# Splitting an expert's first overflow block over two steps of a mixture-of-experts loop

## The chip, the cores and the metric

One core of one Trainium2 chip runs the whole program. The number that counts is the device time of one execution in microseconds (us); lower is better. Engines are named as the profile names them: PE (TensorE, matrix products), DVE (VectorE), ACT (ScalarE), POOL (GpSimd), SP (SyncE, which here only issues the weight transfers).

## What is computed

One decoder layer on 256 tokens of width 1024: a mixer of three kinds of attention, a layer norm, then a mixture of experts (top 4 of 32) and a second layer norm. The change touches the experts alone:

```python
D_MODEL = D_EXPERT = 1024; SEQ = 256; N_EXPERTS = 32; TOP_K = 4      # all float32

def moe_ffn(h, router_w, router_b, w_gu, b_gu, w_dn, b_dn):
    logits = h @ router_w + router_b
    top_logit, top_e = lax.top_k(logits, TOP_K)
    top_w = softmax(top_logit)
    # for every expert e, over the tokens that chose it:
    gu = x @ w_gu[e] + b_gu[e]                      # 1024 -> 2048
    gate = minimum(gu[:, :1024], 7.0)
    up = clip(gu[:, 1024:], -7.0, 7.0)
    act = gate * sigmoid(1.702 * gate) * (up + 1.0)
    y = act @ w_dn[e] + b_dn[e]                     # 1024 -> 1024
    out[tokens] += y * w                            # weighted, added to each token's row
```

The weights of one expert are 8.39 MB (gate and up) and 4.19 MB (down). All 32 are read once, 403 MB in all.

## The kernel before

**Tiling.** An expert has 64 slots for its tokens. An expert chosen by more than 64 tokens has the others done in overflow blocks of 32 slots (`XSLOTS`); `nx[e]` holds how many such blocks expert e needs, and every engine reads it into a register and branches on it. The trace shows two overflow blocks: one for expert 1 (from 298 us) and one for expert 15 (from 741 us), counting from 0.

**Loop.** A pass of the loop (`Fori(0, PAIRS - 1)`, 15 passes) takes two experts: in the first half PE runs the gate-up of expert 2i+1, the gathers for the next two, the down product of 2i, the overflow blocks of 2i, and the transposes of the activations of 2i+1. In the second half it runs the gate-up of 2i+2, the down product of 2i+1, the overflow blocks of 2i+1 (`extra_blocks(1, ...)`, L1130 region), the transposes, and `combine`, which adds the two outputs into four PSUM banks.

**An overflow block on PE** is a gather (`extra_gather`, into PSUM bank PB6), the gate-up (`extra_gate_up_chunk`, 4 chunks, into PB6), transposes of routing weights and activations, the down product (`extra_down_chunk`, 4 chunks), and a combine. DVE makes its one-hot rows (`extra_one_hots`, L1509 to L1520) and its activations (L1494 to L1500 with 64 partitions), ACT copies.

**Weight buffers and the transfer queue.** There are two buffers for gate-up weights (`gu_slot[0]` even experts, `gu_slot[1]` odd ones) and one for down weights (`dn_slot`). SP issues all transfers in one fixed order, expert by expert: gate-up of e+2 (L325), then down of e+1 (L330), each in 4 chunks. A chunk of gate-up e+2 waits for `guc` (the expert's own gate-up has read the chunk of e) and for `xguc` (so have its overflow blocks). A chunk of down e+1 waits for `dn_used` and `xdnc` in the same way. So in the old order an overflow block of e holds the gate-up buffer of e until the next expert's gate-up and the down product of e are through.

**Names in the rows.** `WB` are the weight buffers, `S` (S1, S2) and `K` work tiles and constants in SBUF, `X` the tokens, `PB` the eight PSUM banks. All matrix products are recorded by one helper line, L713 in the kernel before; in the trace every float32 product is two MATMUL rows. L1044 are the transposes of activations, L1087 those of an overflow block, L1538 DVE's copy of the down output.

Of the kernel before, what the change touches and what calls it, by code (L numbers as in the profile page):

```python
# [13 lines left out]
P = 128  # L14
# [40 lines left out]
def hybrid_layer(nc, x, w_in, b_in, pos_k, pos_v, w1_k, w2_k, w1_v, w2_v, g_out, w_out, ln1_g, ln1_b,  # L55
                 router_w, router_b, w_gu, b_gu, w_dn, b_dn, ln2_g, ln2_b, out):
    with ExitStack() as ctx:
# [427 lines left out]
        def _(act):  # L485
# [144 lines left out]
            def extra_slots():  # L630

                act.reg_add(xcount, xcount, 1)
                xc = act.snap(xcount, min_val=1, max_val=96)
                act.wait_ge(s["xga"], xc)
                act.activation(yx[:, 0:KT * XSLOTS], PB[6][:, 0:KT * XSLOTS], ACT.Copy).then_inc(s["xxg"], 1)
# [38 lines left out]
            def extra_blocks(t):  # L674
                n = act.value_load(nx[0:1, t:t + 1] if isinstance(t, int) else nx[0:1, bass.ds(t, 1)], min_val=0,
                                   max_val=MAX_EXTRA)
                with act.If(n > 0):
                    with act.Fori(0, n):
# [8 lines left out]
            combine_weights(1)  # L687
            with act.Fori(0, PAIRS - 1) as i:
                sigmoid(2 * i + 2)
                slots_to_sbuf(0, 6, 2 * i + 3)  # L690
                slots_to_sbuf(1, 4, 2 * i + 4)
                expert_output(0, 2 * i + 1)
                extra_blocks(2 * i)
                act_columns(6, 2 * i + 2)
                sigmoid(2 * i + 3)
                expert_output(1, 2 * i + 2)
                extra_blocks(2 * i + 1)
                act_columns(5, 2 * i + 3)
                combine_weights(i + 2)
            sigmoid(N_EXPERTS)  # L700
            expert_output(0, N_EXPERTS - 1)
            extra_blocks(N_EXPERTS - 2)
            act_columns(6, N_EXPERTS)
            expert_output(1, N_EXPERTS)
            extra_blocks(N_EXPERTS - 1)
# [3 lines left out]
        def _(pe):  # L709
# [357 lines left out]
            def extra_gather(outputs_copied):  # L1067

                pe.reg_add(xcount, xcount, 1)
                xc = pe.snap(xcount, min_val=1, max_val=96)  # L1070

                pe.wait_ge(s["ysb_ok"], outputs_copied + 1)
                pe.wait_ge(s["ysb_dv"], outputs_copied)
                pe.wait_ge(s["xoh"], xc)
                for k in range(KT):
                    for b in range(TB):
                        ins = mm(PB[6][:, XSLOTS * k:XSLOTS * k + XSLOTS], x_sb[:, b, P * k:P * k + P], ohx[:, b, :],
                                 k == 0 and b == 0, b == TB - 1)
                ins.then_inc(s["xga"], 1)
                pe.wait_ge(s["xxg"], xc)  # L1080

# [19 lines left out]
            def extra_blocks(e, t, n):  # L1101

                count = pe.value_load(nx[0:1, t:t + 1] if isinstance(t, int) else nx[0:1, bass.ds(t, 1)], min_val=0,
                                      max_val=MAX_EXTRA)
                with pe.If(count > 0):
                    with pe.Fori(0, count):
                        extra_gather(n)
                        for c in range(GU_CHUNKS):
                            extra_gate_up_chunk(c, e).then_inc(s["xguc"], 1)
                        extra_gate_up_bias(e).then_inc(s["xgu"], 1)  # L1110
                        extra_act_transposes()
                        xc = pe.snap(xcount, min_val=1, max_val=96)
                        pe.wait_ge(s["xctd"], xc)
                        pe.wait_ge(s["xactT"], xc)
                        for c in range(DN_CHUNKS):
                            extra_down_chunk(c).then_inc(s["xdnc"], 1)
                        extra_combine()
                pe.nop()
# [33 lines left out]

            pe.wait_ge(s["actT"], N_EXPERTS - 1)
            gate_up(1, PAIRS, N_EXPERTS)
            pe.wait_ge(s["ct_sb"], PAIRS)
            down(0, PAIRS, N_EXPERTS - 1)
            extra_blocks(0, N_EXPERTS - 2, N_EXPERTS - 1)
            act_transposes(6, N_EXPERTS)
            down(1, PAIRS, N_EXPERTS)
            extra_blocks(1, N_EXPERTS - 1, N_EXPERTS)  # L1160
# [6 lines left out]
        def _(dve):  # L1167
# [372 lines left out]
            def extra_blocks(t, activations_done):  # L1540
                at = (lambda a: a[:, t:t + 1, :]) if isinstance(t, int) else (lambda a: a[:, bass.ds(t, 1), :])
                n = dve.value_load(nx[0:1, t:t + 1] if isinstance(t, int) else nx[0:1, bass.ds(t, 1)], min_val=0,
                                   max_val=MAX_EXTRA)
                with dve.If(n > 0):
# [3 lines left out]
                    with dve.Fori(0, n):  # L1548
                        extra_one_hots()
                        extra_activations(activations_done)  # L1550
# [13 lines left out]
            expert_activations(1)  # L1564
            next_one_hots(0)
            with dve.Fori(0, PAIRS - 1) as i:
# [11 lines left out]
            extra_blocks(N_EXPERTS - 2, N_EXPERTS)  # L1578
            expert_output(1, N_EXPERTS)
            extra_blocks(N_EXPERTS - 1, N_EXPERTS)  # L1580
# [36 lines left out]
```

## Time and profile before

| | |
|---|---|
| median of 3 runs | 1245.11 us (1243.04 to 1245.42) |
| the profiled execution's own time | 1245.07 us |
| its span in the trace | 1243.3 us |
| PE busy | 1115.8 us, 90% |
| DVE, ACT, POOL busy | 266.8, 146.3, 29.7 us |
| moved by DMA | 426.18 MB, 343 GB/s over the span |

The engines' busy times are sums over stages with different limits. The 40 slices show the DMA engines full from about 310 us to the end, but for slices 23 and 24, and empty in part of the stretch before 310 us. The chain that ended last names PE's products with 47% and gate-up transfers with 22% of the span: it goes over PE after each overflow block and over the transfers in between.

### The profile page before, as it was taken

The page shows a single profiled execution, that of the slowest core. Times are in us where ns is not written, and L with a number is a line of the kernel's source. Part 1 is how long each engine was busy: PE and PEld are TensorE (multiplying, and loading weights), DVE is VectorE, ACT ScalarE, POOL GpSimd, SP SyncE. Part 2 cuts the span into 40 slices and gives each one's busy share as a digit, 9 for nine tenths or more (in the row PEclk, how much of TensorE's full clock was granted, in tenths as well). Part 3 has the DMA queues.
Part 4 walks back from the last instruction along what each step waited for, and adds up shares of the span by engine and source line. Part 5 has one row for each costly group of instructions (what it writes and reads, how often), then busy time and mean ns, then how long its engine had stood idle before and what let it go on. Part 6 is the DMA issues. An engine that isn't in the chain of part 4 may idle for free.

```text
span 1243.3 us, 14596 instructions
## 1 busy us (share of the span) xinstructions
PE 1115.8 (90%) x5388; PEld 489.2 (39%) x5389; DVE 266.8 (21%) x767; ACT 146.3 (12%) x309; POOL 29.7 (2%) x52
## 2 busy tenths in 40 slices
PE   7999796998899999999999978999999999999983
PEld 6677445334243333333333333434333332323321
DVE  2353535111112111120211111111212111111113
ACT  2043311100000110000100001000010010100000
POOL 2000410000000000000000000000000000000000
PEclk9999896997999999999999998999999999999997
DMA  9400849630999999999999957999999999999992
GB/s 315 180 1 1 269 196 395 273 137 2 408 418 418 418 418 418 419 418 418 418 418 418 418 243 314 418 418 418 418 418 418 418 419 418 418 418 418 418 414 119
DMA packets 80386, 426.18 MB, mean 343 GB/s; under 512 B 6009, under 2 KB 7594, under 8 KB 47562
## 3 DMA queue, kind: packets, MB, share of 16 engines
q1 hardware_dynamic: 79834, 425.37, 84.7%
q10 hardware_dynamic: 528, 0.48, 0.1%
q8 instruction: 16, 0.26, 0.1%
q14 instruction: 8, 0.07, 0.0%
HBM read 424.78 MB, written 1.05 MB: 343 GB/s over the span
## 4 chain that ended last, share of the span: by engine, by line
PE 49%; DMA 25%; SPq 18%; DVE 3%; issue 3%; ACT 1%; POOL 0%; DVEq 0%; POOLq 0%; ACTq 0%
PE PB L713 47%; DMA WB<-in_w_gate_up_dram 22%; SPq L330 11%; SPq L325 6%; DMA WB<-in_w_down_dram 3%; PE PB L1044 0%; DMA X<-in_x_dram 0%; SPq L334 0%; DVE S L1391 0%; PE PB L720 0%; DVE S L1520 0%; POOL K L476 0%; DVE WB L1285 0%; PE PB L803 0%; DVE S L1497 0%
## 5 line engine op out<-in xcount | busy, mean ns | idle before, releaser
L713 PE MATMUL PB<-WB,S 128*64 128x512 f32 (+5 forms) x3472 | 770.5, 596 | 60.6 <-DMA WB<-in_w_gate_up_dram 54.3
L713 PEld LDWEIGHTS PB<-WB,S 128*64 128x64 f32 (+2 forms) x3472 | 253.2, 140 | 541.7 <-issue 413.4
L1494 DVE TENSOR_SCALAR S<-PB 128x512 f32<-128x512 f32 (+1 forms) x34 | 23.5, 691 | 617.2 <-PE PB L713 617.2
L713 PE MATMUL PB<-S 128*64 128x512 f32 (+5 forms) x464 | 138.2, 580 | 4.7 <-issue 2.3
L656 ACT ACTIVATE S<-S 128x512 f32<-128x512 f32 x32 | 20.2, 630 | 568.7 <-DVE S L1494 568.7
L713 PE MATMUL PB<-S,X 128*128 128x128 f32 (+1 forms) x576 | 76.9, 295 | 9.3 <-DVE S L1520 8.0
L713 PEld LDWEIGHTS PB<-S,X 128*128 128x128 f32 x576 | 73.6, 211 | 23.7 <-issue 21.9
L713 PEld LDWEIGHTS PB<-S 128*64 128x64 f32 (+4 forms) x464 | 53.0, 167 | 74.4 <-issue 67.4
L1538 DVE COPY S<-PB 64x512 f32<-64x512 f32 x32 | 21.9, 684 | 197.6 <-PE PB L713 197.6
L713 PE MATMUL PB<-S,WB 128*128 128x256 f32 (+2 forms) x336 | 63.2, 388 | 0.4 <-ACT S L496 0.4
L713 PEld LDWEIGHTS PB<-S,WB 128*128 128x128 f32 (+1 forms) x336 | 49.1, 177 | 12.4 <-issue 2.1
L713 PE MATMUL PB<-WB 128*32 128x128 f32 (+7 forms) x260 | 44.6, 361 | 5.2 <-DVE WB L1358 3.3
L672 ACT ACTIVATE S<-PB 64x512 f32<-64x512 f32 x32 | 19.0, 594 | 194.9 <-PE PB L713 194.9
L713 PEld LDWEIGHTS PB<-WB 128*64 128x64 f32 (+2 forms) x260 | 27.4, 152 | 18.7 <-issue 13.7
L480 POOL TENSOR_TENSOR K<-K 128x1 f32<-128x1 f32 x2 | 3.0, 1512 | 1041.6 <-DVE K L1413 1041.6
L1044 PEld LDWEIGHTS PB<-K,S 128*128 128x128 f32 x128 | 13.4, 140 | 30.8 <-issue 27.0
L1044 PE MATMUL PB<-K,S 128*128 128x128 f32 x128 | 21.0, 287 | 4.8 <-DVE S L1500 2.8
L1497 DVE SCALAR_TENSOR_TENSOR S<-S 128x512 f32<-128x512 f32 (+1 forms) x34 | 23.5, 691 | 1.2
L1500 DVE TENSOR_TENSOR S<-S 128x512 f32<-128x512 f32 (+1 forms) x34 | 23.5, 691 | 1.2
L1495 DVE TENSOR_SCALAR S<-PB 128x512 f32<-128x512 f32 (+1 forms) x34 | 23.1, 681 | 0.1
L622 ACT ACTIVATE S<-PB 128x512 f32<-128x512 f32 x32 | 19.1, 597 | 32.9 <-PE PB L713 32.9
L1469 DVE TENSOR_SCALAR S<-K 128x64 f32<-128x64 f32 x68 | 16.9, 249 | 20.6 <-PE PB L1049 19.1
(198 smaller groups left out, 338.0 us busy)
## 6 DMA issues: line engine op xcount, KB each, us to landing
WB<-in_w_gate_up_dram SPq DMA_DIRECT2D x128, 2048.0 KB, 22.8
WB<-in_w_down_dram SPq DMA_DIRECT2D x128, 1024.0 KB, 22.9
WB<-in_w_in_dram SPq DMA_DIRECT2D x1, 3088.0 KB, 16.0
WB<-in_w_in_dram SPq DMA_DIRECT2D x1, 3072.0 KB, 20.7
WB<-in_w_in_dram SPq DMA_DIRECT2D x1, 2144.0 KB, 10.8
WB<-in_w_in_dram SPq DMA_DIRECT2D x1, 2048.0 KB, 15.8
WB<-in_w_out_dram SPq DMA_DIRECT2D x2, 1024.0 KB, 10.3
WB<-in_w_out_dram SPq DMA_DIRECT2D x1, 2048.0 KB, 16.8
```

The costliest lines, as they stand in the source:

```text
L325: sp.dma_start(gu_slot[par][:, kk * c:kk * c + kk, :], src[:, kk * c:kk * c + kk, :]).then_inc(s_gul[par][c], 16)
L330: sp.dma_start(dn_slot[:, kk * c:kk * c + kk, :], src[:, kk * c:kk * c + kk, :]).then_inc(s_dnl[par][c], 16)
L622: act.activation(xg[:, 4 * h:4 * h + 4, :].rearrange("p k s -> p (k s)"), PB[bank][:, :], ACT.Copy)\
L656: act.activation(act_sb, gt, ACT.Sigmoid, scale=SWIGLU_ALPHA).then_inc(s["sig"], 1)
L672: act.activation(ysb[64 * e:64 * e + 64, 1, :], PB[7][64:128, :], ACT.Copy).then_inc(s["ysb_ok"], 1)
L713: return mm_(o, l, r, start=start, stop=stop, skip_group_check=True)
L1044: ins = tr(PB[bank][:, P * c:P * c + P], act_sb[:, P * c:P * c + P], ident)
L1494: ts(g, gate, LIMIT, None, ALU.min).then_inc(s[g_ok], 1)
L1495: ts(u, up, LIMIT, -LIMIT, ALU.min, ALU.max).then_inc(s[clip], 1)
L1497: stt(u, u, 1.0, g, ALU.add, ALU.mult).then_inc(s[upg], 1)
L1500: tt(a, u, a, ALU.mult).then_inc(s[done], 1)
L1538: cp(ysb[64 * e:64 * e + 64, 0, :], PB[7][0:64, :]).then_inc(s["ysb_dv"], 1)
```

## The change

The first overflow block of an expert is split. Gather, gate-up and activations now stand at the end of the step in which the expert's own gate-up ran (`start_extra_block`); transposes, down product and combine stay where the whole block stood (`end_extra_blocks`), and blocks after the first are still run there whole. The gather goes to bank PB4 instead of PB6. The main gather's first half moves from PB6 to PB7, so `down` now waits for its copy (`xg_ok`), and the wait for `ct_sb` moves behind it. PE, ACT and DVE each get one more read of `nx` and two more branches per expert. DVE's activations of an expert get a wait for those of the overflow block.

```diff
@@ PE
-            def extra_gather(outputs_copied):
+            def extra_gather():
...
-                pe.wait_ge(s["ysb_ok"], outputs_copied + 1)
-                pe.wait_ge(s["ysb_dv"], outputs_copied)
                 pe.wait_ge(s["xoh"], xc)
...
-                        ins = mm(PB[6][:, XSLOTS * k:XSLOTS * k + XSLOTS], x_sb[:, b, P * k:P * k + P], ohx[:, b, :],
+                        ins = mm(PB[4][:, XSLOTS * k:XSLOTS * k + XSLOTS], x_sb[:, b, P * k:P * k + P], ohx[:, b, :],
...
+            def start_extra_block(e, t, pb6_copied, copies):
+                n = extra_count(t)
+                with pe.If(n > 0):
+                    extra_gather()
+                    pe.wait_ge(s[pb6_copied], copies)
+                    extra_gate_up(e)
+                pe.nop()
+
+            def end_extra_blocks(e, t, outputs_copied):
+                n = extra_count(t)
+                with pe.If(n > 0):
+                    pe.wait_ge(s["ysb_ok"], outputs_copied + 1)
+                    pe.wait_ge(s["ysb_dv"], outputs_copied)
+                    extra_act_transposes()
+                    extra_down()
+                    extra_combine()
+                pe.nop()
+                with pe.If(n > 1):
+                    with pe.Fori(1, n):
+                        extra_gather()
+                        extra_gate_up(e)
                         extra_act_transposes()
+                        extra_down()
                         extra_combine()
                 pe.nop()
...
             combine()
+            start_extra_block(0, 0, "ct_sb", 1)
             with pe.Fori(0, PAIRS - 1) as i:
                 pe.wait_ge(s["actT"], 2 * i + 1)
                 gate_up(1, i + 1, 2 * i + 2)
                 pe.wait_ge(s["ohs"], i + 2)
-                pe.wait_ge(s["ct_sb"], i + 1)
-                gather(0, 6)
+                gather(0, 7)
                 pe.wait_ge(s["g_ok"], 2 * i + 2)
                 gather(1, 4)
+                pe.wait_ge(s["xg_ok"], 2 * i + 3)
                 down(0, i + 1, 2 * i + 1)
                 pe.wait_ge(s["xg_ok"], 2 * i + 4)
-                extra_blocks(0, 2 * i, 2 * i + 1)
+                end_extra_blocks(0, 2 * i, 2 * i + 1)
+                pe.wait_ge(s["ct_sb"], i + 1)
                 act_transposes(6, 2 * i + 2)
+                start_extra_block(1, 2 * i + 1, "actT", 2 * i + 2)
                 gate_up(0, i + 2, 2 * i + 3)
                 down(1, i + 1, 2 * i + 2)
-                extra_blocks(1, 2 * i + 1, 2 * i + 2)
+                end_extra_blocks(1, 2 * i + 1, 2 * i + 2)
                 act_transposes(5, 2 * i + 3)
                 weight_transposes()
                 pe.wait_ge(s["ysb_ok"], 2 * i + 3)
                 pe.wait_ge(s["ysb_dv"], 2 * i + 2)
                 combine()
+                start_extra_block(0, 2 * i + 2, "ct_sb", i + 2)
@@ DVE
             def expert_activations(n):
+                dve.wait_ge(s["xact"], dve.snap(dve.snap(xcount, min_val=0, max_val=96) + 1, min_val=1, max_val=97))
                 dve.wait_ge(s["gu"], n)
...
             with dve.Fori(0, PAIRS - 1) as i:
                 expert_activations(2 * i + 2)
                 expert_output(0, 2 * i + 1)
-                extra_blocks(2 * i, 2 * i + 2)
+                end_extra_blocks(2 * i, 2 * i + 2)
                 next_expert_rows(0, 2 * i + 1)
+                start_extra_slots(2 * i + 1)
+                start_extra_block(2 * i + 1, 2 * i + 2)
                 expert_activations(2 * i + 3)
                 expert_output(1, 2 * i + 2)
-                extra_blocks(2 * i + 1, 2 * i + 3)
+                end_extra_blocks(2 * i + 1, 2 * i + 3)
                 next_expert_rows(1, 2 * i + 2)
+                start_extra_slots(2 * i + 2)
                 next_one_hots(i + 1)
+                start_extra_block(2 * i + 2, 2 * i + 3)
```

ACT is split in the same way: it copies the gathered rows (`extra_slots`) and takes the sigmoid in `start_extra_block`, after `act_columns`, and the other copies in `end_extra_blocks`. SP is unchanged.

**PE, first half of a pass, before.** Behind the down product of the even expert (PB7) come the read of `nx`, the branch, and the whole overflow block; its gate-up is the 32 products into PB6.

```order
L713 MATMUL PB7<-WB,S2 64x512 x16
L1140 REGISTER_ALU
L1103 ISA
L1103 TENSOR_LOAD nx
L1103 ISA x2
L1105 COMPARE_AND_BRANCH
L1106 UNCONDITIONAL_BRANCH
L1069 ISA
L713 MATMUL PB6<-S2,X 128x32 x16
L713 MATMUL PB6<-WB,S2 32x512 x32
L713 MATMUL PB6<-S1,S2 32x512 x4
L1083 ISA
```

**PE, middle of a pass, after.** Behind the transposes of the odd expert's activations (L1062), and ahead of the next expert's gate-up (PB4, last row):

```order
L1062 MATMUL PB6<-K,S2 128x128 x4
L1129 ISA
L1129 TENSOR_LOAD nx
L1129 ISA x2
L1135 COMPARE_AND_BRANCH
L1087 ISA
L731 MATMUL PB4<-S2,X 128x32 x16
L731 MATMUL PB6<-WB,S2 32x512 x32
L731 MATMUL PB6<-S1,S2 32x512 x4
L1135 UNCONDITIONAL_BRANCH
L1027 REGISTER_ALU
L731 MATMUL PB4<-WB,S2 64x512 x2
```

The gate-up of the odd expert's overflow block has moved ahead of the next expert's gate-up and of its own expert's down product.

**DVE, second half of a pass, before**: the read of `nx` and the one-hot rows follow the copy of the odd expert's own down output.

```order
L1538 COPY S2<-PB7 64x512
L1542 TENSOR_LOAD nx
L1542 ISA x2
L1544 COMPARE_AND_BRANCH
L1545 TENSOR_SCALAR K<-K 128x2
L1546 COPY K<-K 128x2
L1547 REGISTER_ALU
L1548 UNCONDITIONAL_BRANCH
L1509 ISA
L1514 REGISTER_ALU
L1515 TENSOR_SCALAR K<-K 128x2
L1518 TENSOR_SCALAR S2<-K 128x32
```

**DVE, first half of a pass, after**: they follow the small operations for the next expert's bias rows (L1523, L1519), which themselves follow the copy of the even expert's down output.

```order
L1523 TENSOR_SCALAR K<-K 128x1
L1519 TENSOR_SCALAR S2<-K 128x64
L1588 REGISTER_ALU
L1588 TENSOR_LOAD nx
L1588 ISA x2
L1595 COMPARE_AND_BRANCH
L1596 ISA
L1596 TENSOR_SCALAR K<-K 128x2
L1597 ISA
L1597 COPY K<-K 128x2
L1598 ISA
L1559 REGISTER_ALU
```

So the odd expert's one-hot rows are made half a pass earlier, behind the copy of the expert before it.

## Rows read from the trace of the kernel before

**Rows 1.** The page's 40 slices of the span: GB/s moved by DMA.

```profile
GB/s 315 180 1 1 269 196 395 273 137 2 408 418 418 418 418 418 419 418 418 418 418 418 418 243 314 418 418 418 418 418 418 418 419 418 418 418 418 418 414 119
```

**Rows 2.** Windows: us, busy time by engine, PE clock, DMA share, GB/s.

```profile
276.50:309.50 33.00, 28.53 (x136) 13.60 (x136) 5.87 (x18) 1.61 (x3) 0.00 (x0) 0.82 0.00 1
...
320.00:733.00 413.00, 385.54 (x1832) 144.29 (x1834) 64.95 (x164) 37.32 (x65) 0.00 (x0) 1.00 1.02 418
...
735.00:752.00 17.00, 12.54 (x64) 8.22 (x64) 3.21 (x14) 0.98 (x2) 0.00 (x0) 0.70 0.00 0
```

**Rows 3.** PE timeline around expert 15's block: start, us, what [idle before, releaser].

```profile
711.48 7.15 PE L713 MATMUL PB<-WB,S 128*64 128x512 f32 x32
...
730.12 7.04 PE L713 MATMUL PB<-WB,S 128*64 128x512 f32 x32
741.14 6.84 PE L713 MATMUL PB<-S,X 128*128 128x32 f32 x32 [3.98 <-DVE S L1520]
...
760.98 0.44 PE L1087 MATMUL PB<-K,S 128*128 128x128 f32 x2 [3.08 <-DVE S L1500]
...
793.63 6.66 PE L713 MATMUL PB<-WB,S 128*64 128x512 f32 x30
```

**Rows 4.** SP's transfer issues around both blocks (L325 gate-up, L330 down weights).

```profile
309.75 6.42 SPq L325 DMA_DIRECT2D WB<-in_w_gate_up_dram  x4
322.54 4.28 SPq L330 DMA_DIRECT2D WB<-in_w_down_dram  x4
```

```profile
752.12 5.50 SPq L325 DMA_DIRECT2D WB<-in_w_gate_up_dram  x4
764.49 3.47 SPq L330 DMA_DIRECT2D WB<-in_w_down_dram  x4
...
795.88 3.76 SPq L330 DMA_DIRECT2D WB<-in_w_down_dram  x3
```

**Rows 5.** PE timeline: the loop's start, expert 1's block, a pass behind it, the end.

```profile
241.22 13.95 PE L713 MATMUL PB<-WB,S 128*64 128x512 f32 x64
...
269.60 0.66 PE L1044 MATMUL PB<-K,S 128*128 128x128 f32 x4 [1.92 <-issue]
270.19 15.65 PE L713 MATMUL PB<-WB,S 128*64 128x512 f32 x64
...
298.42 7.00 PE L713 MATMUL PB<-S,X 128*128 128x32 f32 x32 [4.00 <-DVE S L1520]
...
319.53 0.44 PE L1087 MATMUL PB<-K,S 128*128 128x128 f32 x2 [3.08 <-DVE S L1500]
```

```profile
352.49 7.09 PE L713 MATMUL PB<-WB,S 128*64 128x512 f32 x32
359.51 0.66 PE L1044 MATMUL PB<-K,S 128*128 128x128 f32 x4
...
387.12 13.95 PE L713 MATMUL PB<-WB,S 128*64 128x512 f32 x64
...
402.72 3.84 PE L713 MATMUL PB<-S,X 128*128 128x128 f32 x32
406.49 7.09 PE L713 MATMUL PB<-WB,S 128*64 128x512 f32 x32
...
1201.54 3.60 PE L713 MATMUL PB<-WB,S 128*64 128x512 f32 x16
```

**Rows 6.** DVE timeline ahead of expert 15's block: output copy, last one-hot rows.

```profile
737.20 0.69 DVE L1538 COPY S<-PB 64x512 f32<-64x512 f32 x1 [4.13 <-PE PB L713]
...
740.07 0.92 DVE L1520 TENSOR_SCALAR S<-K 128x32 f32<-128x32 f32 x4
```

**Rows 7.** Instruction queue: whole span, 200 to 345 us; then every queue of 345 to 1195 us.

```profile
q8 instruction: 16, 0.26, 0.1%
```

```profile
q8 instruction: 6, 0.10, 0.3%
```

```profile
q1 hardware_dynamic: 59630, 346.55, 99.3%
```

More of the change, by code:

```diff
@@ L634, in extra_slots @@
                 act.wait_ge(s["xga"], xc)
-                act.activation(yx[:, 0:KT * XSLOTS], PB[6][:, 0:KT * XSLOTS], ACT.Copy).then_inc(s["xxg"], 1)
+                act.activation(yx[:, 0:KT * XSLOTS], PB[4][:, 0:KT * XSLOTS], ACT.Copy).then_inc(s["xxg"], 1)
             def extra_sigmoid():
@@ L672, in expert_output, with extra_count, start_extra_block, end_extra_blocks @@
                 act.activation(ysb[64 * e:64 * e + 64, 1, :], PB[7][64:128, :], ACT.Copy).then_inc(s["ysb_ok"], 1)
-            def extra_blocks(t):
-                n = act.value_load(nx[0:1, t:t + 1] if isinstance(t, int) else nx[0:1, bass.ds(t, 1)], min_val=0,
-                                   max_val=MAX_EXTRA)
-                with act.If(n > 0):
-                    with act.Fori(0, n):
+            def extra_count(t):
+                return act.value_load(nx[0:1, t:t + 1] if isinstance(t, int) else nx[0:1, bass.ds(t, 1)], min_val=0,
+                                      max_val=MAX_EXTRA)
+            def start_extra_block(t):
+                n = extra_count(t)
+                with act.If(n > 0):
+                    extra_slots()
+                    extra_sigmoid()
+                act.nop()
+            def end_extra_blocks(t):
+                n = extra_count(t)
+                with act.If(n > 0):
+                    extra_act_copy()
+                    extra_outputs()
+                act.nop()
+                with act.If(n > 1):
+                    with act.Fori(1, n):
                         extra_slots()
@@ L1080, in extra_gather, with extra_gate_up, extra_down @@
                 pe.wait_ge(s["xxg"], xc)
+            def extra_gate_up(e):
+                for c in range(GU_CHUNKS):
+                    extra_gate_up_chunk(c, e).then_inc(s["xguc"], 1)
+                extra_gate_up_bias(e).then_inc(s["xgu"], 1)
+            def extra_down():
+                xc = pe.snap(xcount, min_val=1, max_val=96)
+                pe.wait_ge(s["xctd"], xc)
+                pe.wait_ge(s["xactT"], xc)
+                for c in range(DN_CHUNKS):
+                    extra_down_chunk(c).then_inc(s["xdnc"], 1)
             def extra_act_transposes():
@@ L1099, in extra_combine, with extra_count @@
                         mm(acc(b, h)[:, :], CTx[64 * h:64 * h + 64, b, :], yx[64 * h:64 * h + 64, :], False, False)
[L1101 to L1110, printed above, removed]
-                        extra_act_transposes()
[L1112 to L1116, printed above, removed]
+            def extra_count(t):
+                return pe.value_load(nx[0:1, t:t + 1] if isinstance(t, int) else nx[0:1, bass.ds(t, 1)], min_val=0,
+                                     max_val=MAX_EXTRA)
+            def start_extra_block(e, t, pb6_copied, copies):
+                n = extra_count(t)
+                with pe.If(n > 0):
[4 more added lines that the diff above has]
+            def end_extra_blocks(e, t, outputs_copied):
+                n = extra_count(t)
+                with pe.If(n > 0):
[9 more added lines that the diff above has]
+                        extra_gate_up(e)
+                        extra_act_transposes()
+                        extra_down()
                         extra_combine()
@@ L1547, in extra_blocks, with start_extra_block, end_extra_blocks @@
                     dve.reg_add(xexperts, xexperts, 1)
-                    with dve.Fori(0, n):
+                    extra_one_hots()
+                dve.nop()
+            def start_extra_block(t, activations_done):
+                n = extra_count(t)
+                with dve.If(n > 0):
+                    extra_activations(activations_done)
+                dve.nop()
+                dve.nop()
+            def end_extra_blocks(t, activations_done):
+                n = extra_count(t)
+                with dve.If(n > 1):
+                    with dve.Fori(1, n):
                         extra_one_hots()
@@ L1564, in _ @@
             expert_activations(1)
+            start_extra_slots(0)
             next_one_hots(0)
+            start_extra_block(0, 1)
             with dve.Fori(0, PAIRS - 1) as i:
```

35 lines of the change are left out of this document (22 added, 13 removed).

## The prediction, as it stood before the run

> **What bounds the kernel now.** I read the 40 slices first. From slice 10 on the DMA engines are full at 418 GB/s, except in slices 23 and 24 [rows 1]. Windows set around the holes show the rest: 418 GB/s from 320 to 733 us and, by the slices, the same behind 754.5 us; nothing from 276.5 to 309.5 and from 735 to 752 us [rows 2]. So the end is set by the weight stream: its volume at 418 GB/s, plus the time in which it stands still. One expert's weights (12.58 MB) take 30.1 us, 20.1 of them gate-up (8.39 MB) and 10.0 down. PE has slack: unhindered it does a pass of two experts in 406.49 - 352.49 = 54.0 us [rows 5] against 60.2 for the stream.
>
> Both holes belong to the overflow blocks. SP issues the gate-up load of expert e+2 only when the block of e has read the buffer: at 309.75 and 752.12 us [rows 4], 11.3 and 11.0 us after the block's gather began [rows 3, 5]; data flow about 1.1 us after an issue. By edges of the windows I take the stream as dead from 275.3 to 310.8 us (35.5 us, expert 1) and from 734.0 to 753.2 us (19.2 us, expert 15).
>
> **What the change does at expert 15.** It moves the block's gather and gate-up ahead of the gate-up of 16, which starts at 711.48 [rows 3]. All times are in the clock of the old trace.
> - DVE must first make the one-hot rows. From the start of its output copy to the last one takes 740.99 - 737.20 = 3.8 us [rows 6]; two small operations for the bias rows now stand between, some 0.5 us. The down product of 14 ends 0.6 us of transposes before 711.48 and its copy starts near 711.0, so PE can gather from 715.4. PE is idle 4 us, as now (3.98). I cost this at the same slow gather as today: the clock in 735 to 752 us is 0.70 on average [rows 2], so part of it ran at 1.2 GHz, and the same idle should bring the same.
> - Gather to end of gate-up takes 760.98 - 3.08 - 741.14 = 16.8 us [rows 3]: PE is free at 732.2.
> - SP issues the load for 17 at 715.4 + 11.0 = 726.4. The stream is still busy until 734.0, so this hole closes, and the load is through at 754.1.
> - But down of 16 also waits (`xdnc`) for the block's down product. PE: gate-up of 16 without waits 402.72 - 387.12 = 15.6 [rows 5], down of 15 7.0, a copy of 0.7 [rows 6] that the block's transposes must now await. They start at 755.5 instead of 760.98, 5.5 us earlier. The issue of down 16 moves from 764.49 [rows 4] to 759.0, its data to 760.1: a new hole of 6.0 us. Hidden now: the wait of 3.08 us for DVE's activations, and the DMA-paced part of the gate-up.
> - Next late is down of 17, issued once down 16 has run: 795.88 [rows 4] minus 5.5, data at 791.5. The stream, from 760.1 on with 30.1 us of work, is out at 790.2: 1.3 us more.
> In the kernel before, the stream reaches that load at 753.2 + 20.1 + 30.1 = 803.4. **Gain 803.4 - 791.5 = 11.9 us**, not the 19.2 us of the hole: the limit becomes PE's own path over the block. Further on PE takes 27.0 us for an expert against 30.1, so no hole follows.
>
> **At expert 1.** The down product of 0 ends 1.92 us before 269.60 [rows 5]; with 4.3 us of DVE work and 0.3 for its slower first pass PE gathers from 272.3. The block runs 319.53 - 3.08 - 298.42 = 18.0 us, to 290.3; gate-up 15.6, down 7.0, copy 0.7: transposes at 313.6 instead of 319.53. That is 5.9 earlier; 1.5 of it because the gate-up of 2 ran partly at half clock behind the 1.92 us stop (15.65 us for its 64 products, against 13.95 at 387.12). The load of 3 is issued at 272.3 + 11.3 = 283.6 (data 284.7 to 304.8), down of 2 at 322.54 - 5.9 = 316.6 (data 317.7 to 347.8, with gate-up of 4). Down of 3 waits for down of 2, at 352.49 [rows 5] plus the 2.25 us from start to issue seen at 793.63 and 795.88 [rows 3, 4]: 354.7 - 5.9 + 1.1 = 349.9. Before, the stream is there at 310.8 + 50.2 = 361.0. **Gain 11.1 us**.
>
> **What it costs.** The moved waits are free: down waits for ACT's copy of the first gather half (a bank's copy, 0.7 us on DVE [rows 6]), which the second half of the 3.84 us gather covers [rows 5]; without that cover it would cost 0.7 us per pass, within the slack. PE gets one more read of `nx` and two more branches per expert. In the steady passes the present read and branch cost PE nothing visible: down starts at 352.49 and lasts 7.09, transposes follow at 359.51 [rows 5]. In the first pass the same place shows 1.92 us of "issue" [rows 5]. Bounds for an added branch are thus 0 and 1.92 us; below nothing is excluded, since nothing is removed. I take 0 in steady state (the nearest row, and the slack covers small stops), 1 us in each of the two catch-up stretches, and 3 us at the end, where the code behind the loop is run once and two added skips stand ahead of the last down product. Sum: 11.9 + 11.1 - 2 - 3 = 18, of which I drop 1 for ends rounded in my favour. 1245.07 (the profiled execution, which lies within 0.1 us of the median) - 17 = **1228 us**.
>
> **The rule that speaks against it.** PE's code in the loop grows: by the built order 290 matrix products before, 446 after, since gather, gate-up, down and combine now stand twice per expert. With two MATMUL and two weight loads for each float32 product that is about 1160 and 1790 instructions. The instruction queue q8 brings 16 packets in the span, 6 of them between 200 and 345 us, and none from 345 to 1195 us, where only q1 moved anything [rows 7]: the old loop was loaded once and stayed. Whether the new one does, no row shows. The Trainium skill ("Runtime: NRT & Kernel Launch", Instruction fetch mechanics) says that PE holds 2048 instructions in 16 KiB blocks of 256, refilled first in, first out with sequential prefetch, and that a taken branch to a block that isn't there stalls for the fetch. By that page, as an estimate, the new loop covers all eight blocks and the prefetched ninth would push out the first; the trace agrees with the page on the block size (0.26 MB in 16 packets).
>
> **Rivals.**
> 1. *The loop no longer stays loaded and the skips stop PE, slower.* The place is the branches over unused code: five per pass (one long one behind each of the two down products, one over the unused first half behind each set of transposes, one back to the loop's start). PE alone would finish at 358 + 15p us: the first gate-up of the loop starts at 241.2 and the down product behind the last one at 1201.5 [rows 5], 43.6 before the end; between them 15 passes of p, the last gate-up of 15.6, and an estimated 29 for each block (its 18.0 and 16.8, and 12 for transposes, down, combine and the idle ahead). At p = 59.1 this is the old time, so it decides from 5.1 us of stops per pass. Three stops of 1.92 give 59.8 and 1255 us; five 63.6 and 1312; with a half-clock gate-up behind two of them (1.7 each) 67.0 and 1363. For it: code 1.5 times as long, and a first pass that shows the stop. 
> 2. *Small stops eat the gain.* One refetch per pass and 3 us of idle with its half clock makes p 58.7 to 59.3, where PE and no longer the stream is the bound: 1238 to 1248.
> 3. *Both holes close wholly*: 35.5 + 19.2 = 55 us less, 1190 to 1210. For it: gate-up loads are two thirds of the stream. Against it: `xdnc` still ties the down weights to the late half of the block.
>
> **How the numbers follow.** Forecast (gain 7 to 31, 1214 to 1238): 0.55. The low end is both blocks at full clock and no branch cost, the high end both added branches visible. Rival 1: 0.28, spread over 1255 to 1360. Rival 2: 0.12. Rival 3: 0.05. The range from 1213 to 1300 holds the forecast, rival 2 and nearly half of rival 1, together 0.8. A change of 0.2% (2.5 us) is about what a measurement of this kernel can tell from none. Faster: 0.55 + 0.05 + 0.05 of rival 2; same 0.03; slower 0.32.
>
> **What would show it.** Right: gate-up load of 3 issued near 284 and of 17 near 726; holes of about 9 and 13 us around expert 1, and of 6 to 8 us near 755 (all later times shifted by the first gain); 418 GB/s elsewhere; q8 with no packets through the loop, or one or two per pass; PE waits for gate-up chunks again before the end. Wrong: q8 with dozens of packets, "issue" stops of 2 us and more behind the down products, a DMA rate under 418 GB/s throughout. If the holes close to 5 us or less in sum, the PE path was costed too long.

## The result, and the profile after

The changed kernel takes 1417.38 us (median of 4, 1415.85 to 1421.1) against 1244.07 for the kernel before beside it: ratio 1.140, 95% interval 1.138 to 1.143. The forecast was 1228 with a range of 1213 to 1300; the time is 173 us longer than before and outside it. The profiled execution has a span of 1413.9 us and a mean PE clock of 0.89 (0.97 before). Lines have moved: products are L731 (was L713), the transposes of the activations L1062 (L1044) and of the one-hot rows L1067 (L1049), the block's transposes L1114 (L1087), DVE's output copy L1585 (L1538) and block one-hot rows L1565 (L1520), the last activation step L1545 (L1500).

The page's 40 slices answer [rows 1]:

```profile
GB/s 323 112 1 94 237 380 286 120 238 359 326 385 321 390 339 381 327 388 313 388 319 382 195 264 295 378 338 369 347 360 356 357 359 356 361 351 364 340 189 131
```

There is no plateau at 418 GB/s left. The blocks show as dips (120 and 238 GB/s in slices 8 and 9, 195 and 264 in slices 23 and 24), but the slices between them run at 313 to 390. So the stream no longer sets the end. The page says who does: its queue row (packets, MB, share), the chain that ended last by engine, and the costliest group (busy, mean ns | idle before, releaser).

```profile
q8 instruction: 147, 2.41, 0.8%
...
PE 81%; issue 14%; DVE 3%; DMA 1%; ACT 1%; SPq 0%; POOL 0%; DVEq 0%; POOLq 0%; ACTq 0%
...
L731 PE MATMUL PB<-WB,S 128*64 128x512 f32 (+5 forms) x3472 | 820.0, 631 | 156.6 <-issue 153.2
```

The instruction queue brought 147 packets, where it brought 16 [rows 7]. PE stood for 153.2 us ahead of its products without waiting for any semaphore, and 14% of 1413.9 us, 198 us, of the chain is such time.

The PE timeline shows where. It starts at the overflow block of expert 1 and runs through the first two steady passes (start, us, what, [idle before, releaser]), for [rows 5]:

```profile
271.55 0.63 PE L1062 MATMUL PB<-K,S 128*128 128x128 f32 x4 [2.06 <-issue]
...
274.80 7.03 PE L731 MATMUL PB<-S,X 128*128 128x32 f32 x32 [2.62 <-DVE S L1565]
...
315.60 0.43 PE L1114 MATMUL PB<-K,S 128*128 128x128 f32 x2 [0.98 <-DVE S L1585]
...
353.52 3.84 PE L731 MATMUL PB<-S,X 128*128 128x128 f32 x32
357.29 7.09 PE L731 MATMUL PB<-WB,S 128*64 128x512 f32 x32
366.35 0.63 PE L1062 MATMUL PB<-K,S 128*128 128x128 f32 x4 [1.97 <-issue]
372.05 15.38 PE L731 MATMUL PB<-WB,S 128*64 128x512 f32 x64 [5.07 <-issue]
...
406.54 16.89 PE L731 MATMUL PB<-WB,S 128*64 128x512 f32 x64 [5.99 <-issue]
...
425.08 3.84 PE L731 MATMUL PB<-S,X 128*128 128x128 f32 x32
...
438.01 0.63 PE L1062 MATMUL PB<-K,S 128*128 128x128 f32 x4 [2.07 <-issue]
443.65 15.41 PE L731 MATMUL PB<-WB,S 128*64 128x512 f32 x64 [5.01 <-issue]
...
477.38 15.62 PE L731 MATMUL PB<-WB,S 128*64 128x512 f32 x64 [5.18 <-issue]
...
494.64 3.84 PE L731 MATMUL PB<-S,X 128*128 128x128 f32 x32
```

A pass now takes 425.08 - 353.52 = 71.6 us, where PE alone took 54.0 and the stream 60.2. The 17.6 us are three stops, 1.97 + 5.07 + 5.99 = 13.0, and the two gate-ups behind the long ones, of which a part runs at half clock: 15.38 and 16.89 us (granted clock 0.90 and 0.82) where 13.95 is the full-clock time [rows 5], 1.4 + 2.9. All three lie where a skip jumps over unused code: behind the first down product, behind the transposes of the odd expert's activations, and at the loop's end. Behind the second down product there are skips too, and no stop shows. The next pass has the same three and takes 69.6 us. Rival 1's formula, 358 + 15p, gives 1402 to 1432 for these two passes; the span is 1413.9.

The middle of the run as one window, 345 to 1150 us (us, busy time of PE, its weight loads, DVE, ACT and POOL, then PE clock, DMA share, GB/s), where [rows 2] had 418 GB/s:

```profile
345.00:1150.00 805.00, 662.67 (x2970) 251.11 (x2966) 109.52 (x281) 59.76 (x104) 0.00 (x0) 0.89 0.86 342
```

And PE's groups in that window: first the products, then the transposes (busy, mean ns of one | idle before, releaser).

```profile
L731 PE MATMUL PB<-WB,S 128*64 128x512 f32 (+1 forms) x2190 | 520.4, 649 | 114.8 <-issue 113.7 <-ACT S L647 0.6 <-ACT S L635 0.5
...
L1062 PE MATMUL PB<-K,S 128*128 128x128 f32 x88 | 14.1, 283 | 22.9 <-issue 22.9
```

In the kernel before, the same group of products has its idle time from the weights, 49.0 of 50.0 us, and none from issue:

```profile
L713 PE MATMUL PB<-WB,S 128*64 128x512 f32 (+1 forms) x2626 | 576.8, 601 | 50.0 <-DMA WB<-in_w_gate_up_dram 49.0 <-ACT S L647 0.6 <-ACT S L635 0.5
```

**The theory from here** (A): the larger PE loop is fetched anew in each pass, and the skips wait for it. **Rivals**: (B) the added reads of `nx` and branches themselves cost this, wherever the code lies; (C) the moved waits or the split itself set the pass.

### The profile page after: what moved, and what is told of

Same layout as the page of the kernel before. It is cut to its first block, busy times and chain, and to the rows that moved or that the text cites. A ratio compares the mean times of both kernels' runs of the same rounds, so it can differ in the third digit from the quotient of the medians.

```text
span 1413.9 us, 15234 instructions
## 1 busy us (share of the span) xinstructions
PE 1167.7 (83%) x5388; PEld 510.7 (36%) x5389; DVE 267.3 (19%) x767; ACT 146.2 (10%) x309; POOL 29.7 (2%) x52
## 3 DMA queue, kind: packets, MB, share of 16 engines
q8 instruction: 147, 2.41, 0.8%
## 4 chain that ended last, share of the span: by engine, by line
PE 81%; issue 14%; DVE 3%; DMA 1%; ACT 1%; SPq 0%; POOL 0%; DVEq 0%; POOLq 0%; ACTq 0%
PE PB L731 78%; PE PB L1062 1%; DMA WB<-in_w_in_dram 1%; DVE S L1436 0%; PE PB L1067 0%; POOL K L476 0%; DVE S L1565 0%; SPq L304 0%; DVE WB L1330 0%; DVEq L1588 0%; DVE S L1585 0%; PE PB L821 0%; SPq L312 0%; DVE K L1454 0%; PE PB L962 0%
## 5 line engine op out<-in xcount | busy, mean ns | idle before, releaser
L731 PE MATMUL PB<-WB,S 128*64 128x512 f32 (+5 forms) x3472 | 820.0, 631 | 156.6 <-issue 153.2
L731 PEld LDWEIGHTS PB<-WB,S 128*64 128x64 f32 (+2 forms) x3472 | 274.9, 150 | 668.8 <-issue 660.6
L731 PE MATMUL PB<-S 128*64 128x512 f32 (+5 forms) x464 | 138.8, 582 | 3.2 <-ACT S L652 1.4
L731 PE MATMUL PB<-S,X 128*128 128x128 f32 (+1 forms) x576 | 77.2, 296 | 6.2 <-DVE S L1565 4.8
L731 PEld LDWEIGHTS PB<-S,X 128*128 128x128 f32 x576 | 73.9, 212 | 19.3 <-issue 12.2
L731 PEld LDWEIGHTS PB<-S 128*64 128x64 f32 (+4 forms) x464 | 53.4, 168 | 73.2 <-issue 64.6
L731 PE MATMUL PB<-S,WB 128*128 128x256 f32 (+2 forms) x336 | 61.8, 383 | 0.7 <-ACT S L496 0.5
L1585 DVE COPY S<-PB 64x512 f32<-64x512 f32 x32 | 21.9, 683 | 202.3 <-PE PB L731 202.3
L731 PEld LDWEIGHTS PB<-S,WB 128*128 128x128 f32 (+1 forms) x336 | 47.8, 174 | 12.4 <-issue 2.1
L1062 PE MATMUL PB<-K,S 128*128 128x128 f32 x128 | 21.0, 288 | 36.1 <-issue 33.1
L731 PE MATMUL PB<-WB 128*32 128x128 f32 (+7 forms) x260 | 44.7, 362 | 5.2 <-DVE WB L1403 3.3
L1062 PEld LDWEIGHTS PB<-K,S 128*128 128x128 f32 x128 | 13.7, 143 | 62.6 <-issue 58.8
L731 PEld LDWEIGHTS PB<-WB 128*64 128x64 f32 (+2 forms) x260 | 27.5, 152 | 18.7 <-issue 13.7
L660 ACT ACTIVATE S<-PB 128x512 f32<-128x512 f32 x32 | 19.1, 597 | 45.1 <-PE PB L1062 45.1
L1545 DVE TENSOR_TENSOR S<-S 128x512 f32<-128x512 f32 (+1 forms) x34 | 23.5, 691 | 1.2
L622 ACT ACTIVATE S<-PB 128x512 f32<-128x512 f32 x32 | 19.1, 597 | 33.0 <-PE PB L731 33.0
```

The costliest lines, as they stand in the source:

```text
L622: act.activation(xg[:, 4 * h:4 * h + 4, :].rearrange("p k s -> p (k s)"), PB[bank][:, :], ACT.Copy)\
L660: act.activation(actT[:, :, :].rearrange("p c s -> p (c s)"), PB[bank][:, :], ACT.Copy)\
L731: return mm_(o, l, r, start=start, stop=stop, skip_group_check=True)
L1062: ins = tr(PB[bank][:, P * c:P * c + P], act_sb[:, P * c:P * c + P], ident)
L1545: tt(a, u, a, ALU.mult).then_inc(s[done], 1)
L1585: cp(ysb[64 * e:64 * e + 64, 0, :], PB[7][0:64, :]).then_inc(s["ysb_dv"], 1)
```

## The experiments

A count is used in them: PE instructions by the built program, with four for a float32 product (two MATMUL, two weight loads) and two for a transpose. The loop has 1163 before and 1790 after. The queue's packets are 16 KB each (2.41 MB in 147). I count the code in blocks of 256 instructions; that is what the Trainium skill says ("Runtime: NRT & Kernel Launch", Instruction fetch mechanics) of 16 KiB, and the 16 KB packets agree with it.

**e1: only the first block, split.** The loops for second and later blocks are left out on PE; with these inputs they never run. The split stays, the loop shrinks to 1168 instructions.

```diff
 def end_extra_blocks(e, t, outputs_copied):
     ...
     pe.nop()
-    with pe.If(n > 1):
-        with pe.Fori(1, n):
-            extra_gather()
-            extra_gate_up(e)
-            extra_act_transposes()
-            extra_down()
-            extra_combine()
-    pe.nop()
```

> The changed kernel without PE's code for overflow blocks after the first (it is never run with these inputs, where no expert has more than one). The loop's code falls from about 1790 to 1168 PE instructions; reads of nx and the first branches stay. Theory A (the loop's code no longer stays loaded): the stops of 5 to 6 us per half pass vanish, q8 brings nothing from about 345 us to the end of the loop, and the time is 1222 to 1233 us, which is also where the split alone should land. Theory B (the added reads and branches themselves stop PE, four reads instead of two per pass): 1390 us or more. Theory C (the split order makes PE wait for DVE or ACT in every pass): unchanged at 1417.

Measured: 1223.07 us (4 runs), ratio 0.982 [0.977, 0.986]. The stops are gone: 0 packets on q8 in the window 345 to 1150 us, and the products wait for weights again:

```profile
L731 PE MATMUL PB<-WB,S 128*64 128x512 f32 (+1 forms) x2672 | 586.8, 603 | 40.7 <-DMA WB<-in_w_gate_up_dram 39.6 <-ACT S L647 0.6 <-ACT S L635 0.5
```

So (C) falls: split, waits and reads are as in the changed kernel. What is missing is unused code and the test `n > 1` ahead of it, one skip per expert; whether that skip matters is for e4 and e5. This kernel also shows the forecast's own terms. PE's timeline at the loop's start and around both blocks:

```profile
239.61 5.94 PE L731 MATMUL PB<-S 128*128 128x512 f32 x8
245.48 13.95 PE L731 MATMUL PB<-WB,S 128*64 128x512 f32 x64
...
277.25 7.04 PE L731 MATMUL PB<-S,X 128*128 128x32 f32 x32 [4.73 <-DVE S L1557]
...
318.06 0.43 PE L1114 MATMUL PB<-K,S 128*128 128x128 f32 x2 [0.98 <-DVE S L1577]
...
708.85 7.04 PE L731 MATMUL PB<-S,X 128*128 128x32 f32 x32 [4.42 <-DVE S L1557]
...
750.60 0.43 PE L1114 MATMUL PB<-K,S 128*128 128x128 f32 x2 [0.98 <-DVE S L1577]
```

SP's issues of gate-up and down weights, as in [rows 4]:

```profile
288.62 5.72 SPq L325 DMA_DIRECT2D WB<-in_w_gate_up_dram  x4
...
320.70 2.95 SPq L330 DMA_DIRECT2D WB<-in_w_down_dram  x4
...
720.22 6.66 SPq L325 DMA_DIRECT2D WB<-in_w_gate_up_dram  x4
...
753.25 4.63 SPq L330 DMA_DIRECT2D WB<-in_w_down_dram  x4
```

Windows in the holes and between them:

```profile
280.50:289.50 9.00, 8.53 (x46) 4.88 (x50) 0.00 (x0) 0.38 (x1) 0.00 (x0) 0.55 0.00 0
312.20:321.60 9.40, 7.86 (x51) 2.77 (x51) 2.17 (x7) 1.36 (x3) 0.00 (x0) 1.00 0.01 2
345.00:745.00 400.00, 374.82 (x1808) 144.64 (x1806) 67.99 (x172) 35.99 (x62) 0.00 (x0) 0.98 1.02 416
747.50:754.00 6.50, 4.95 (x32) 1.76 (x32) 1.40 (x5) 1.36 (x3) 0.00 (x0) 0.92 0.00 0
```

**e2: the old kernel with unused code.** The kernel before, plus a branch never taken over two more gate-ups, once per half pass: 1743 instructions, and nothing split or moved.

```diff
 (kernel before, in the extra blocks' code, once per expert)
+with pe.If(count > 5):
+    for c in range(GU_CHUNKS):
+        extra_gate_up_chunk(c, e)
+    extra_gate_up_bias(e)
+    for c in range(GU_CHUNKS):
+        extra_gate_up_chunk(c, e)
+    extra_gate_up_bias(e)
```

> The kernel before, order untouched, with a never-taken branch of 288 PE instructions after each pair of overflow blocks (1743 instructions in the loop instead of 1163, over 8 blocks of 256). Theory A: about nine packets of q8 per pass, PE's pass near 65 to 71 us, 1335 to 1425 us. Theories B and C: 1244 us, since only one more branch per half pass is run and no order changes.

Measured: 1445.43 us (2 runs), ratio 1.161 [1.155, 1.167], 20 us above what I expected at most. The direction is (A)'s: unused code, with one skip per half pass over it, makes the old kernel slower than the changed one. PE's timeline has the same kind of stop, here the longest behind a down product, and the queue row of 345 to 1150 us shows the fetches:

```profile
365.85 7.09 PE L713 MATMUL PB<-WB,S 128*64 128x512 f32 x32
380.39 1.12 PE L1044 MATMUL PB<-K,S 128*128 128x128 f32 x4 [7.46 <-issue]
...
407.66 0.66 PE L1044 MATMUL PB<-K,S 128*128 128x128 f32 x4 [1.98 <-issue]
```

```profile
q8 instruction: 95, 1.56, 0.8%
```

**e4: the old kernel with more reads and branches, little code.** This is (B) by itself: per half pass two more reads of `nx`, each with a branch not taken; 1247 instructions.

```diff
+for _ in range(2):
+    again = pe.value_load(nx[...], min_val=0, max_val=MAX_EXTRA)
+    with pe.If(again > 5):
+        extra_gate_up_bias(e)
+    pe.nop()
```

> The kernel before with two more reads of nx and two more never-taken short branches per half pass on PE (1247 instructions in the loop). Theory A: 1243 to 1246 us, no stop on PE. Theory B: four more reads and branches per pass at the 1 to 2 us of the stops seen give 1260 to 1330 us.

Measured: 1247.82 us (8 runs), ratio 1.0030 [1.0009, 1.0052], 2 us above my range. The total alone proves little, since the stream hides up to 60.2 - 54.0 = 6.2 us per pass. PE's own pass decides: where it has no wait for weights (from one first down product to the next) it takes 409.73 - 355.74 = 54.0 us, as before. But where PE waits for weights anyway, one small stop per pass does show, 0.4 to 0.9 us behind the second down product, against my "no stop on PE"; in 345 to 1150 us, with no packet on q8, they add up to:

```profile
L1044 PE MATMUL PB<-K,S 128*128 128x128 f32 x104 | 17.1, 287 | 7.2 <-issue 7.1
```

The changed kernel has 113.7 + 22.9 us of issue idle in its window. So (B) falls as the cause: four reads and branches more per pass cost 0.9 us of PE's time at most where their code is held.

**e3, e6: the changed kernel with shorter code.** The second copy of the block is saved by turning the loop around: one body ends a block and begins the next. It does as many blocks as the changed kernel's. 1602 instructions. e3 has some 100 unused instructions ahead of the loop besides, e6 none.

```diff
-    with pe.If(n > 0):
-        waits, act_transposes, down, combine
-    with pe.If(n > 1):
-        with pe.Fori(1, n):
-            gather, gate_up(e), act_transposes, down, combine
+    with pe.If(n > 0):
+        with pe.Fori(0, n) as j:
+            waits, act_transposes, down, combine
+            with pe.If(j < n - 1):
+                gather, gate_up(e)
```

> The changed kernel with the code for later blocks folded: one loop over all blocks of an expert, transposes, down and combine first, then gather and gate-up if another block follows. Every block count still works. 1602 PE instructions in the loop, and about 100 unused ones ahead of it, so that it lies in 7 blocks of 256. Theory A: it fits, 1222 to 1235 us. Theories B and C: 1390 us or more.

> The rotated loop with nothing unused ahead of it. By my count it ends within 20 instructions of the boundary between its seventh and eighth block, the runtime's own instructions ahead being unknown. Theory A1: either 1225 to 1232 us with no q8 packets in the loop, or 1390 to 1430 with nine per pass, nothing in between. Theory A2: about 1229.

Measured: e3 1229.32 us (4 runs), ratio 0.988 [0.984, 0.992]; e6 1226.76 (2 runs), 0.986 [0.981, 0.990]. For e6 my count left both outcomes open; its time is that of a loop that stays loaded. No stop in the steady passes; e3's PE timeline at the places where the changed kernel stops:

```profile
411.17 0.66 PE L1062 MATMUL PB<-K,S 128*128 128x128 f32 x4
411.76 13.95 PE L731 MATMUL PB<-WB,S 128*64 128x512 f32 x64
...
438.77 13.95 PE L731 MATMUL PB<-WB,S 128*64 128x512 f32 x64
```

From 345 to 1150 us only q1 moved data in e3. A loop 1.4 times the old length, with the split's reads and waits and one skip fewer per expert than in the changed kernel, stays loaded.

**e5: e3, moved by some 50 instructions.** The same loop to the instruction, with half the unused code ahead of it. By my count the loop touches seven blocks of 256 in e3, and eight in e5, since its start slips below a boundary. For e6 the count ended too near a boundary to tell; its time puts it at seven.

```diff
 with pe.If(never > 5):
-    for _ in range(6):
+    for _ in range(3):
         extra_gate_up_bias(0)
```

> The rotated loop with its 1602 instructions unchanged, but with about 50 unused instructions ahead of it instead of 100. Its start slips from just behind to just ahead of a boundary of 256 instructions, so it touches 8 blocks instead of 7 (with the one fetched ahead 9 instead of 8). Theory A1 (PE holds 8 blocks of 256, replaced in the order of use or of loading, counted in whole blocks): nine packets of q8 per pass and 1390 to 1430 us. Theory A2 (it is the number of instructions that counts, 1602 against a limit somewhere up to 1743): same as the rotated loop, about 1229 us.

Measured: 1451.15 us in the profiled execution, against 1242.81 before. (Its second timing was 6459.59 us; it has no trace, I can't explain it, and give no ratio.) The stops are back, in the queue row of 345 to 1150 us and in PE's timeline:

```profile
q8 instruction: 94, 1.54, 0.9%
```

```profile
399.27 0.66 PE L1062 MATMUL PB<-K,S 128*128 128x128 f32 x4 [2.22 <-issue]
...
412.77 2.82 PE L731 MATMUL PB<-WB,S 128*64 128x512 f32 x5 [9.19 <-issue]
418.48 14.18 PE L731 MATMUL PB<-WB,S 128*64 128x512 f32 x58 [2.90 <-issue]
```

This is the sharpest of the runs, though it is one execution: work, order, waits, reads and branches of the loop are those of e3. Only its place in the code differs, and it costs over 220 us. So neither the skip that e1 and e3 lack nor (B) or (C) is needed for the stops.

**e7: e2 with half the unused code.** 1455 instructions, seven blocks.

```diff
 with pe.If(count > 5):
     for c in range(GU_CHUNKS):
         extra_gate_up_chunk(c, e)
     extra_gate_up_bias(e)
-    for c in range(GU_CHUNKS):
-        extra_gate_up_chunk(c, e)
-    extra_gate_up_bias(e)
```

> The kernel before with half of the unused code of the earlier run (144 instructions after each pair of overflow blocks, 1455 in the loop, 7 blocks). Theory A1: nothing is fetched again and the time is that of the kernel before, 1242 to 1248 us. If instead the length of a skipped stretch stops PE, it lies between 1244 and 1445, near 1340.

Measured: 1250.68 us (8 runs), ratio 1.0044 [1.0023, 1.0066], 3 us above my range; no packets from 345 to 1150 us. The rise from 1251 to 1445 lies between 1455 and 1743 instructions, where a cost by length would have put this run near 1340. The interval overlaps that of e4, so the two can't be told apart. One visible part of what it lost is a stop where code is run for the first time, ahead of the last down product:

```profile
1218.74 1.11 PE L1044 MATMUL PB<-K,S 128*128 128x128 f32 x4 [5.18 <-issue]
```

**e8: what limits the split once the code is short.** In e1, PE idles 4.7 and 4.4 us ahead of each gather for DVE's one-hot rows, and the gather then takes 7.04 us. So DVE makes these rows ahead of the output copy. This is e1's kernel (later blocks left out on PE), with one line moved:

```diff
 (DVE loop)
     expert_activations(2 * i + 2)
+    start_extra_slots(2 * i + 1)
     expert_output(0, 2 * i + 1)
     ...
-    start_extra_slots(2 * i + 1)
```

> The split without later blocks' code on PE (1223 us), and DVE makes the odd expert's one-hot rows before it waits for the even expert's down product (this order would deadlock if two neighbouring experts had blocks, which these inputs don't have). Theory 'PE's path sets the gain': the idle of 4.7 and 4.4 us ahead of the gathers goes, with part of the half-clock stretch; PE is 5 to 8 us earlier at each block's end, holes of 9.75 and 6.9 us shrink by as much, and the time is 1209 to 1216 us. Rival 'the stream sets it' (gate-up volume once the first hole is filled): within 2 us of 1223.

Measured: 1204.84 us (4 runs), ratio 0.968 [0.965, 0.972]; 4 us below the expected range, and 18 us below e1. In the two profiled executions, 25 us apart, 5.1 us of the difference lie ahead of the loop (it starts at 240.40 against 245.48), which the moved line doesn't touch. PE's timeline:

```profile
267.29 3.66 PE L731 MATMUL PB<-S,X 128*128 128x32 f32 x32
...
304.49 0.43 PE L1114 MATMUL PB<-K,S 128*128 128x128 f32 x2 [0.98 <-DVE S L1577]
...
690.04 3.66 PE L731 MATMUL PB<-S,X 128*128 128x32 f32 x32
```

Besides the idle time, the gather fell from 7.04 to 3.66 us, since PE reached it at full clock: the granted clock was 1.00 in it, and 0.50 in e1's. Of the three holes in e1's windows one of some 11 us is left; the rest of the run is dense:

```profile
297.80:308.00 10.20, 8.65 (x50) 2.93 (x50) 2.97 (x8) 1.61 (x4) 0.00 (x0) 0.92 0.01 2
309.00:1179.00 870.00, 819.71 (x3943) 307.92 (x3934) 142.71 (x366) 78.84 (x137) 0.00 (x0) 1.00 1.01 416
```

**e9: both mends in a kernel that leaves nothing out.** e6's turned loop, with DVE making the rows early unless the expert before has overflow blocks of its own:

```diff
 (e6's kernel, DVE loop)
     expert_activations(2 * i + 2)
+    n = extra_count(2 * i)
+    with dve.If(n < 1):
+        start_extra_slots(2 * i + 1)
     expert_output(0, 2 * i + 1)
     ...
-    start_extra_slots(2 * i + 1)
+    n = extra_count(2 * i)
+    with dve.If(n > 0):
+        start_extra_slots(2 * i + 1)
```

> A version that keeps every block count and every neighbourhood of blocks: the rotated loop on PE (7 blocks of 256 instructions) and, on DVE, the odd expert's one-hot rows made ahead of the wait for the even expert's down product where the even expert has no overflow block, else where the change has them. If both findings add up, as PE's resident code and PE's path over the block: 1203 to 1212 us, no q8 packets between 340 and 1150 us, no idle ahead of the two gathers. If DVE's added reads and branches matter, or the two do not add, about 1227.

Measured: 1218.97 us (6 runs), ratio 0.980 [0.977, 0.984], faster than before but 7 us above my range. From 345 to 1150 us there is no packet and no issue stop. The miss is in the first pass, in code run for the first time, as in e7; PE's timeline:

```profile
271.50 0.63 PE L1062 MATMUL PB<-K,S 128*128 128x128 f32 x4 [2.00 <-issue]
...
323.65 1.11 PE L1062 MATMUL PB<-K,S 128*128 128x128 f32 x4 [4.74 <-issue]
...
1187.20 1.09 PE L1062 MATMUL PB<-K,S 128*128 128x128 f32 x4 [5.22 <-issue]
```

These are 12.0 us of stops at skips. In a window around each of them (266 to 273, 318 to 325 and 1175 to 1190 us) the instruction queue brought one packet, so I read them as skips whose target was just being fetched. In e8's shorter code PE's timeline shows no issue stop at any of these places. But e6, with the same PE code, has the first and the third too (2.10 and 4.93 us); there the first cost nothing, since the gather waited for DVE's rows anyway, and at the second place it did not stop, though a packet came between 318 and 326 us. What is new against e6 is thus the first stop in the open, the second, and the slower groups behind them (the gather 5.05 us instead of 3.66, the combine 5.79 instead of 3.60): 2.0 + 0.5 + 1.4 + 4.7 + 2.2, some 11 us, an estimate from these rows. Why e6 passed the second place without a stop is open.

## Why the prediction was wrong

- **The bound of the kernel before** (the stream, with two holes): right. Where the code stays loaded, 416 GB/s came back in the long stretches outside the holes (e1, e8).
- **The split at expert 1**: right, even in the slow kernel, where the gather starts at 274.80 and the transposes at 315.60. In e1 the loop starts 4.3 us later than before (245.48 against 241.22 [rows 5]), because the combine ahead of the loop began 1.9 us later (239.61 against 237.70) and ran mostly at half clock (5.94 us against 3.60; granted clock 0.60 in it, against 1.00). That isn't the split's: e7, with the old order, has 239.12 and 5.96. Less that shift, the gather is at 273.0 (272.3 forecast), the load of 3 at 284.3 (283.6), the transposes at 313.8 (313.6). The windows bound the holes from below at 9.0 and 9.4 us; the forecast had 9.4, and 12.9 + 2.1 for the second with its successor. The second came out smaller: the load ahead of it ran from 290 to 311.5 us at 388 GB/s, not at the 418 of its forecast 20.1 us.
- **The split at expert 15**: right. Gather to load issue 720.22 - 708.85 = 11.4 us (11.0 taken), gather to transposes 41.8 us (755.5 - 715.4 = 40.1 taken), idle ahead of the gather 4.42 (4 taken), a slow gather of 7.04 as taken, a hole of at least 6.5 us (6.0).
- **The gain of the split alone**: e1 gained 21.5 us against 17 forecast, by the medians of the same runs. I had taken off 3 us for skips at the end, and e1's short code has no issue stop there; the rest of the difference is not assigned. With one block per expert at most in these inputs, e3 and e6, which leave nothing out, gained 15 and 16 us, 1 to 2 below the forecast.
- **The step that failed** is the one in "What it costs": bounds of 0 and 1.92 us for an added branch, and "I take 0 in steady state (the nearest row, and the slack covers small stops)". The row was nearly right for a loop that stays loaded: e4 shows at most 0.9 us per pass for four reads and branches more. It says nothing of one that doesn't, where three stops took 13.0 us of the 71.6 us pass and the slow products behind them 4.3, and the instruction counts, 1160 to 1790, stood one paragraph below. I treated the two as separate matters, a price and a rule that speaks against it, when the first hangs on the second.
- **Rival 1 had the mechanism and the places (stops show at three of its five), but a term too small.** It took the 1.92 us seen in the first pass as the price of a stop: 5 x 1.92 and two slow gate-ups, p = 67.0. Measured were 1.97, 5.07 and 5.99 us and p = 71.6. A reading that fits the changed kernel, and isn't shown: 1.92 us was only the visible rest of a fetch behind a down product, and behind 0.6 us of transposes, or at the loop's end, more of it shows. The other slow kernels don't follow it (7.46 us behind a down product in e2, 1.42 behind the transposes in e5). With the measured stops and its own 1.7 us for each slow gate-up it would have come to 54.0 + 13.0 + 3.4 = 70.4, or 358 + 15 x 70.4 = 1414 us; that this meets the span so closely is partly luck, as passes of 69.6 and 71.6 us are 30 us apart by it. Its upper end of 1360 was set by the same small row.
- **"After one load nothing was fetched again, and a cache that replaces block for block would refetch only the one or two that collide"** spoke against rival 1 and lowered its chance to 0.28. The runs show otherwise: with one block too many, as much as the whole loop is fetched in each pass. The changed kernel has 98 packets in 805 us, that is 98 / (805 / 71.6) = 8.7 per pass, for a loop that touches eight blocks by my count.

Not settled: why the long stops differ between kernels with equal numbers of packets (5.99 us in the changed kernel, 7.46 in e2, 9.19 in e5), so that e2 is slower than the changed kernel with less code; and e5's second timing. That eight blocks are held is inferred from the times and the packets, not read from any row, and so is the link from a single fetch to a single stop.

## What to carry to other kernels

Unused code in a loop isn't free: before adding a branch with a body to one, count the instructions of the whole loop on the engine, with four for each float32 product, and look at the instruction queue in a steady stretch. If it moves nothing now and the loop grows by half, the question is not what the branch costs but whether the loop still stays loaded; here the answer turned a gain of 21 us into a loss of 173. If it falls out, fold copies of a body into one before giving up the idea, and price the skips by the whole span of what such loops show, 1.4 to 9.2 us for one stop here and 13 in a pass, not by the 1.92 us of a single row.

## What the runs showed of the hardware

- **PE's code is held or lost as a whole.** Loops that touch up to seven blocks of 256 instructions brought 0 packets in 345 to 1150 us (before, e1, e3, e4, e6, e7, e8, e9); loops that touch eight brought 98, 95 and 94 (after, e2, e5). That is what one would see if eight blocks were held, one ahead of the running one was always fetched, and the oldest was dropped; no run tells other orders of dropping from this. The Trainium skill ("Runtime: NRT & Kernel Launch", Instruction fetch mechanics) gives PE 2048 instructions, which is eight blocks, refilled first in, first out with sequential prefetch; the traces agree with the size. It also speaks of two cache lines and a two-page window; on PE no run here fits that, since loops of seven blocks ran through with no fetch.
- **The place matters as much as the length.** The same 1602 instructions took 1229 and 1451 us, some 50 instructions apart. The block counts take in some 50 instructions that stand ahead of the kernel's own; I didn't see these, but e3 and e6 both fit only if there are 24 to 59 of them, so this number is fitted to the runs.
- **Four reads and branches more per pass, with their code held, cost PE 0 to 0.9 us** (e4), the latter only in passes in which it waits for weights.
- **First passage is priced too**: 2.0 to 5.2 us for a skip in code not yet fetched (e7, e9), though one such place in e6 shows no stop.
- **A gather of 16 products (32 MATMUL rows) took 3.66 us when PE came to it without a pause, and 7.04 behind 4 us of idle** (e8 against e1), at a granted clock of 1.00 and 0.50, the two levels of 2.4 and 1.2 GHz. An idle stretch ahead of a short group on a critical path costs nearly the group's length again.
